# A two-block transformer kernel: the ends of the first block's layers worked by token tile, with a new order of weight loads

## The reference, cut to what matters

```python
for l in range(DEPTH):                       # DEPTH = 2
    h = rms_norm(x, pre_norm_g[l])           # x * rsqrt(mean(x*x) + 1e-6) * g
    u = jnp.einsum('bsd,de->bse', h, w_in[l])
    u_mla, u_sb, u_moba, u_conv, u_gate = jnp.split(u, SPLITS, axis=-1)
    ...                                      # MLA, stick-breaking and MoBA attention, a convolution of 31 taps
    y = jnp.concatenate([o_a, o_b, o_c, o_d], axis=-1) * jax.nn.silu(u_gate)
    y = jnp.einsum('bse,ed->bsd', y, w_out[l])
    x = x + rms_norm(y, post_norm_g[l])
```

```python
c_act = jax.nn.silu(c)
mods = jnp.split(c_act @ w_ada[i] + b_ada[i], 6, axis=-1)
u = x * (1.0 + sc1) + sh1
```

## Time and profile before

| | us |
|---|---|
| median of 3 runs (lowest, highest) | 1155.36 (1154.93, 1157.49) |
| the profiled execution | 1159.07 |
| its span, first to last instruction | 1156.6 |
| TensorE busy in the span | 1077.7 (93%) |
| VectorE busy | 448.8 (39%) |
| ScalarE busy | 167.5 (14%) |
| mean granted clock of TensorE | 0.968 |

### The profile page before, as it was taken

The page is one execution under the profiler, slowest core; times in us unless marked ns, Lnnn a source line. Parts: engine busy times, 40 slices in busy tenths (PEclk is TensorE's granted clock), DMA queues, the critical chain, the costliest instruction groups (busy, mean ns, idle before and its releaser), DMA issues. The chain is left out here.

```text
span 1156.6 us, 11866 instructions
## 1 busy us (share of the span) xinstructions
PE 1077.7 (93%) x4214; PEld 739.2 (64%) x4214; DVE 448.8 (39%) x1111; ACT 167.5 (14%) x402; POOL 25.1 (2%) x42
## 2 busy tenths in 40 slices
PE   3999994999999998997999999999999799999993
PEld 2758752758756857645666666678885466666661
DVE  2495625495725242537333333363322600000005
ACT  1124211124211231101000000002231000000000
POOL 2000000000000000000200000000000000000000
PEclk9999997999998999998999999979999899999997
DMA  6554454554465353345866555625332344444440
GB/s 246 218 207 181 161 216 161 218 195 182 168 218 218 146 218 146 108 183 190 303 231 239 218 218 220 232 93 182 109 116 103 114 177 154 164 153 145 145 145 36
DMA packets 29165, 204.58 MB, mean 177 GB/s; under 512 B 3423, under 2 KB 3460, under 8 KB 5453
## 3 DMA queue, kind: packets, MB, share of 16 engines
q1 hardware_dynamic: 26796, 191.60, 44.6%
q0 software_dynamic: 2336, 12.58, 2.9%
HBM read 203.11 MB, written 1.05 MB: 177 GB/s over the span
## 5 line engine op out<-in xcount | busy, mean ns | idle before, releaser
L1196 PE MATMUL bank<-hT,raw 128*128 128x256 f32 x2176 | 482.1, 380 | 2.9 <-DMA raw<-units_dram 2.4
L1196 PEld LDWEIGHTS bank<-hT,raw 128*128 128x128 f32 x2176 | 411.8, 190 | 77.0 <-issue 16.9
L1437 PE MATMUL bank<-raw,arena 128*128 128x512 f32 x512 | 224.6, 592 | 0.0
L1437 PEld LDWEIGHTS bank<-raw,arena 128*128 128x128 f32 x512 | 97.3, 190 | 109.7 <-issue 108.1
L1048 DVE TENSOR_TENSOR arena<-arena 128x512 f32<-128x512 f32 x32 | 23.8, 743 | 324.1 <-ACT arena L588 324.1
L1206 PE MATMUL bank<-raw,yT 128*128 128x512 f32 x224 | 99.4, 602 | 2.3 <-DVE yT L1108 2.0
L996 DVE SCALAR_TENSOR_TENSOR ada<-raw,cact,ada 128x256 f32 (+1 forms) x168 | 82.3, 490 | 6.0
L1206 PE MATMUL bank<-raw,hT 128*128 128x512 f32 (+1 forms) x192 | 76.7, 559 | 2.4 <-DVE hT L794 2.4
L1206 PEld LDWEIGHTS bank<-raw,yT 128*128 128x128 f32 x224 | 42.8, 193 | 55.3 <-issue 52.9
L588 ACT ACTIVATE arena<-bank 128x512 f32<-128x512 f32 x32 | 19.1, 597 | 397.8 <-PE bank L1196 397.8
L1206 PEld LDWEIGHTS bank<-raw,hT 128*128 128x128 f32 x192 | 37.2, 195 | 40.4 <-issue 34.7
(11 more groups left out here) (250 smaller groups left out, 714.1 us busy)
## 6 DMA issues: line engine op xcount, KB each, us to landing
raw<-units_dram SPq DMA_DIRECT2D x180, 1024.0 KB, 4.8
arena<-ln_rows_dram POOLq DMA_DIRECT2D x4, 1024.0 KB, 5.9
arena<-ada_rows_dram POOLq DMA_DIRECT2D x1, 2048.0 KB, 7.4
arena<-att_line_dram POOLq DMA_DIRECT2D x1, 2048.0 KB, 14.7
arena<-small_dram POOLq DMA_DIRECT2D x2, 896.0 KB, 6.5
xt<-x_dram SPq DMA_DIRECT2D x1, 1024.0 KB, 5.0
arena<-post_g_dram POOLq DMA_DIRECT2D x2, 512.0 KB, 8.8
out_dram<-xt SPq DMA_DIRECT2D x1, 1024.0 KB, 4.0
```

The lines of the kernel that those rows point to most:

```text
L1196: mm = pe.matmul(b[:, c * S:(c + 1) * S], raw[:, s, k * 256 + c * P:k * 256 + (c + 1) * P], act_t[:, k, :], start=(k == 0), stop=(k == KC ...
L1437: mm = pe.matmul(G[2 * h + t][:], hid[:, k, c, t * P:(t + 1) * P], raw[:, n % SLOTS, c * D + h * 512:c * D + (h + 1) * 512], start=False, ...
```

## The change

The order of units changes, and SP loads in another order at the start:

```diff
-ORDER = "wwawawwawwawawwa" "wawawawa" "wwawwa"
+ORDER = "wwwawwawwawawawa" "wawawawa" "awwwwa"
...
-            sp.dma_start(xt[:], x.rearrange("a (t p) d -> p (a t) d", p=P)).then_inc(x_in, 16)
-            sp.dma_start(kst[:], consts).then_inc(const_in, 16)
-            sp.dma_start(oneh[:], onehot).then_inc(rel_in, 16)
-            sp.dma_start(cact[:], ccol).then_inc(rel_in, 16)
+            sp.dma_start(cact[:], ccol).then_inc(ccol_in, 16)
+            sp.dma_start(xt[:, 0, :], x[0, 0:P, :]).then_inc(x_in[0], 16)
+            sp.dma_start(ident, consts[:, K_ID:K_ID + P]).then_inc(ident_in, 16)
+            sp.dma_start(xt[:, 1, :], x[0, P:S, :]).then_inc(x_in[1], 16)
+            sp.dma_start(oneh[:], onehot).then_inc(rel_in, 16)
             for s in range(SLOTS):
                 sp.dma_start(raw[:, s, :], units[s, :, :]).then_inc(landed[s], 16)
+            sp.dma_start(kst[:, P:], consts[:, P:]).then_inc(const_in, 16)
```

POOL's loads of the layer vectors (col, sm, gb) now wait for the first layer's `xs`; the gain of the first norm has a small tensor of its own, `pre`. The root on VectorE becomes four small instructions behind a root by ACT, one tile at a time:

```diff
+            def root_of(ssq, root):
+                ch.do(dve.tensor_scalar(neg[:], ssq, -0.5 / D, -0.5 * EPS, ALU.mult, ALU.add))
+                ch.do(dve.reciprocal(inv[:], root))
+                ch.sync()
+                ch.do(dve.tensor_scalar(err[:], inv[:], inv[:], neg[:], ALU.mult, ALU.mult))
+                ch.sync()
+                ch.do(dve.tensor_scalar(rst[:], err[:], 1.5, inv[:], ALU.add, ALU.mult))
+                ch.sync()
...
-                ada_unit(l, 0)
...
+                ada_unit(l, 0)
                 ada_unit(l, 1)
...
+                for t in range(NT):
+                    wait_output(dve, l, t)
+                    dve.wait_ge(osq_ready.sem, osq_ready.at(l, t + 1))
+                    ch.do(dve.tensor_tensor(xs[:, t, :], OY[t], gb[:], ALU.mult))
+                    dve.wait_ge(sso_ready.sem, sso_ready.at(l, t + 1))
+                    root_of(ssy[:, t:t + 1], root_y[:, t:t + 1])
+                    dve.scalar_tensor_tensor(xt[:, t, :], xs[:, t, :], rst[:], xt[:, t, :], ALU.mult,
+                                             ALU.add).then_inc(x_new.sem, 1)
```

`OY[t]` is one tile's output over two neighbouring banks. TensorE does the last two output units, the transposes and the first two units by tile, and multiplies zeros while it waits:

```diff
+            def zero_work(b, n):
+                for _ in range(n):
+                    pe.matmul(b[:], zeros[:, 0:P], zeros[:], start=True, stop=True)
...
+            def last_units(l):
+                for u in (U_O2, U_O3):
+                    wait_landed(pe, T1 * l, u)
+                for t in range(NT):
+                    for i, u in enumerate((U_O2, U_O3)):
+                        for k in range(4):
+                            mm = pe.matmul(OB[i][t][:], yT[:, 4 + k, t * P:(t + 1) * P],
+                                           raw[:, u % SLOTS, k * 512:(k + 1) * 512], start=False, stop=(k == 3))
+                        if t == 1:
+                            mm.then_inc(used[u % SLOTS], 1)
+                        elif i == 1:
+                            mm.then_inc(o_ready.sem, 1)
+
+            pe.wait_ge(zeros_ready, 1)
+            zero_work(G[0], 10)
...
             with pe.Fori(0, DEPTH) as l:
-                pe.wait_ge(xs_ready.sem, xs_ready.at(l, 2))
...
+                zero_work(A[0], 18)
+                first_transposes(l, 0)
+                first_units(l, 0)
+                first_transposes(l, 1)
+                first_units(l, 1)
```

More of the change, by code:

```diff
@@ L395, in _ @@
             for l in range(1, DEPTH):
+                pre_columns(l)
                 layer_vectors(l)
@@ L588, in relu_group @@
                 act.activation(relu[:, k], A[k][:], ACT.Relu).then_inc(relu_ready.sem, 1)
-            stage_input(0)
+            act.wait_ge(coef_ready.sem, coef_ready.at(0, 1))
+            for t in range(NT):
+                act.wait_ge(t0_ready, 2 * t + 1)
+                for c in range(4):
+                    act.activation(hT[:, c, t * P:(t + 1) * P], UB[t][0][:, c * P:(c + 1) * P], ACT.Identity,
+                                   scale=ucoef[:, 0, 0, c:c + 1], bias=ucoef[:, 0, 1, c:c + 1]).then_inc(u0_act, 1)
             act.wait_ge(lowp_ready, 1)
@@ new lines, in _ @@
+                    dve.tensor_scalar(xs[:, t, :], xt[:, t, :], rst[:], None, ALU.mult).then_inc(xs_ready.sem, 1)
+                dve.wait_ge(pre_in.sem, pre_in.at(l, 16))
+                for t in range(NT):
+                    dve.wait_ge(htp_ready.sem, htp_ready.at(l, 2 * t + 2))
+                    for i in range(4):
+                        c = 4 + i
+                        dve.tensor_scalar(hT[:, c, t * P:(t + 1) * P], HB[t][1][:, i * P:(i + 1) * P],
+                                          pre[:, c:c + 1], None, ALU.mult).then_inc(ht_dve.sem, 1)
@@ L1051, in _ @@
             coefficients(0)
-            stage_input(0)
+            for t in range(NT):
+                dve.wait_ge(t0_ready, 2 * t + 2)
+                for i in range(4):
+                    c = 4 + i
+                    dve.tensor_scalar(hT[:, c, t * P:(t + 1) * P], UB[t][1][:, i * P:(i + 1) * P], ucoef[:, 0, 0, c:c + 1],
+                                      ucoef[:, 0, 1, c:c + 1], ALU.mult, ALU.add).then_inc(u0_dve, 1)
             gate_rows(0)
@@ L1232, in values, with first_units @@
                 pe.matmul(o[:, c + P:c + S], v1, probsT[:, j % 2, S:384], start=False, stop=True).then_inc(pv_ready.sem, 1)
-            pe.wait_ge(rel_in, 32)
+            def zero_work(b, n):
+                for _ in range(n):
+                    pe.matmul(b[:], zeros[:, 0:P], zeros[:], start=True, stop=True)
+            def first_units(l, t):
+                for half, u in enumerate((U_MLA0, U_MLA1)):
+                    wait_landed(pe, T1 * l, u)
+                    for k in range(4):
+                        ht = ht_dve if half else ht_act
+                        pe.wait_ge(ht.sem, ht.at(l, 4 * t + k + 1))
+                        mm = pe.matmul(A[t][:, 0:MLA_IN], hT[:, 4 * half + k, t * P:(t + 1) * P],
+                                       raw[:, u % SLOTS, k * 512:k * 512 + MLA_IN],
+                                       start=(half == 0 and k == 0), stop=(half == 1 and k == 3))
+                    if t == NT - 1:
+                        mm.then_inc(used[u % SLOTS], 1)
@@ new lines, in first_transposes @@
+            def first_transposes(l, t):
+                pe.wait_ge(xs_ready.sem, xs_ready.at(l, t + 1))
+                for q in range(2):
+                    for i in range(4):
+                        c = 4 * q + i
+                        mm = pe.transpose(HB[t][q][:, i * P:(i + 1) * P], xs[:, t, c * P:(c + 1) * P], ident)
+                    mm.then_inc(htp_ready.sem, 1)
+            def last_units(l):
+                for u in (U_O2, U_O3):
+                    wait_landed(pe, T1 * l, u)
+                for t in range(NT):
+                    for i, u in enumerate((U_O2, U_O3)):
+                        for k in range(4):
+                            mm = pe.matmul(OB[i][t][:], yT[:, 4 + k, t * P:(t + 1) * P],
+                                           raw[:, u % SLOTS, k * 512:(k + 1) * 512], start=False, stop=(k == 3))
+                        if t == 1:
+                            mm.then_inc(used[u % SLOTS], 1)
+                        elif i == 1:
+                            mm.then_inc(o_ready.sem, 1)
@@ L1454, in net @@
                 second_product(s, 0, n0 + 1 + 5 * per, GROUPS - 1, 0, True)
-            modulation(0)
-            pe.wait_ge(x_new.sem, 2 * DEPTH + 2)
-            stage_input(0, xt)
+            modulation_columns(0)
+            for t in range(NT):
+                pe.wait_ge(x_new.sem, 2 * DEPTH + t + 1)
+                for q in range(2):
+                    for i in range(4):
+                        c = 4 * q + i
+                        mm = pe.transpose(UB[t][q][:, i * P:(i + 1) * P], xt[:, t, c * P:(c + 1) * P], ident)
+                    mm.then_inc(t0_ready, 1)
+            modulation_rows(0)
             pe.wait_ge(gla_in, 32)
-            pe.wait_ge(u_dve.sem, 4)
+            pe.wait_ge(u0_act, 8)
+            pe.wait_ge(u0_dve, 8)
             for k in range(KC):
-                wait_input(0, k)
                 mm = pe.matmul(A[1][0:16, 0:S], wlow[:, k, :], hT[:, k, :], start=(k == 0), stop=(k == KC - 1))
```

170 lines of the change are left out of this document (83 added, 87 removed).

## The result

The changed kernel takes 1185.26 us (median of 4 runs, 1181.5 to 1185.98) against 1155.14 us for the kernel before beside it (4 runs, 1154.69 to 1157.49): ratio 1.0256, 95% interval 1.0234 to 1.0278. It is slower, as forecast, and by 17 us more than forecast. The profiled execution is 1184.92 us, its span 1183.1 us, against 1156.6 us before: 26.5 us longer.

A forecast was written before the change was run, and what follows sets the result against it. TensorE's work was taken to bound each layer's body, with stops at the start and between layers. -10.2 - 11.4 - 2.6 + 30.4 + 6.4 = +12.6 gave 1171.7 profiled, 1168 us as median; range 1159 to 1175.

The forecast's parts named there:

- Start: Before the first layer's unit CA: it starts at 25.2 instead of 35.41 us, -10.2, bounds -11.6 and -5.4.
- Between the layers: From the output product to the next CA: +18.0 us instead of 29.8, taken as -11.4, bounds -12.5 and -8.5.
- Into the second block: From the columns' start to L1465: 17.0 to 18.0 us instead of 19.3, taken as -2.6, bounds -3.2 and -1.3.
- Order of units, waits: In the layers' bodies, TensorE waits 8.2 (nl), 2.6 (O0), 4.8 us (O2, O3): +30.4 for two layers, 29.3 to 31.5.
- Clock: Half clock behind the new waits in the bodies: 3.2 us a layer, +6.4 in all, 3 to 11.
- From profile to median: The profiled execution before lay 3.7 us above its median; that difference was applied, taking 1171.7 to 1168.
- the ends don't shrink as told: Rival: half clock between the layers and a start gaining only 5.4 us; +23.8, 1179 us. Chance of both 0.07, one 0.15.
- the five bounds: The bounds given with the five summed terms; the likeliest case was said to run from +5 to +24 us.

The follow-up runs named there:

- e2: The changed kernel with the order of units of the kernel before: 1171.38 us, ratio 1.0126.
- e8: The changed kernel with products of zeros ahead of the three waits in each layer's body: 1171.41 us, ratio 1.0146.
- e6: The changed kernel with the mended order of units, and O3's landing waited for only before its own first product: 1141.53 us, ratio 0.9874.
- e12: The kernel before with nothing but the mended order of units: 1153.86 us, ratio 0.9992.
- e1: The kernel before with nothing but the change's new order of units: 1187.32 us, ratio 1.0276.
- e5: The changed kernel with the mended order, VectorE's loop over the layers written out, and O3 waited for only before its own first product: 1135.63 us, ratio 0.9824.
- e11: As e5, but with 6 products of zeros instead of 18 ahead of each layer's first transposes: 1134.84 us, ratio 0.9809.
- e3: The changed kernel with the mended order of units (a2 ahead of V0, a3 unit 9, a10 behind O0): 1150.76 us, ratio 0.995.
- e10: As e7, with POOL's loads of the layer's vectors also held until both xs of that layer are written: 1186.04 us.
- e7: The changed kernel, with VectorE waiting for the next layer's third unit to land before its loop jumps back: 1188.82 us.
- e9: The changed kernel without the 18 products of zeros ahead of each layer's first transposes: 1184.67 us, ratio 1.0239.
- e4: The changed kernel with VectorE's loop over the two layers written out: 1176.59 us, ratio 1.0166.

## Why the prediction was right in its sign and wrong in its size

- *Start*: forecast -10.2, measured 35.41 to 25.70, **-9.7**. The one-hot product came at 7.59 (7.5 forecast), the zeros took 5.75 (3.9 to 7.8) and ended last, as told. (On the 35.41, see the last point.)
- *Between the layers*: forecast -11.4, measured 29.84 to 25.34, **-4.5**. This is the step that failed. "After that VectorE does tile 0's root and scaling" passed over the jump of VectorE's loop, which the change brings onto the path: before, ACT's square had to run there anyway; now the square of tile 0 is done early and VectorE's next instruction is the path. Written out, the stretch is 17.9 us (18.0 forecast before the allowance for the clock). Over the 18.4 of the sum the gap is 5.3 us; half clock behind the longer stop took 2.2, where 0.4 was allowed.
- *Into the second block*: forecast -2.6, measured **-0.35**. The steps went as told (no wait at the L1465 of before, L1560 now), but the clock fell earlier within the columns, 11.27 for 9.34, which the sum left out; where it fell later (e2, e8) the entry is 19.2, -3.7. The term was too large by its own sum as well: 17.0 to 18.0 against 19.3 is -1.3 to -2.3, not -2.6.
- *Order of units, waits*: forecast +30.4. The three waits were forecast at 8.2, 2.6 and 4.8 and measured at 8.12, 2.64 and 4.73, and e8 leaves 15.5 and 14.9 us over the old bodies: **+30.4**. The account through slots and queue was right, and not by luck: counted from CA, VectorE got a2 at +28.3 and a3 at +45.4, and TensorE's transposes went on at +71.8, against +28.5, +45.5 and +71.9. Its heading was not: e2 shows that the wait for O2 and O3 comes also with the old order (5.0 and 5.2), since the products by token tile want O3 earlier and the code waits for both units at once; with the mended order a wait for each unit removes it (e6).
- *Clock*: forecast +6.4 (3 to 11), measured 165.44 + 165.67 less 144.27, 144.17 and 30.4: **+12.3**, of which e8 takes back 12.5. This is the second step that failed. The mechanism was right and the size half: the short stops were put at 0.65 each, and the rows show 1.7 behind 2.64 (O0, 8.83 for 7.13) and 2.7 behind 4.73. Twice the loss is the time at half clock: 3.4 and 5.4 us, longer than the stops themselves.
- *From profile to median*: I carried 3.7 us from the profiled execution of before over to the median. The profiled execution after lies at its median (1184.92 and 1185.26), so this added 4.0 to the miss. That execution of before lies above all its others (1154.69 to 1157.49). The rows show where: its first units ran partly at half pace. First MLA0 and MLA1 of before, then of e12, which has the old code there:

```profile
23.73 11.50 PE L1206 MATMUL bank<-raw,hT 128*128 128x352 f32 x32 [1.17 <-DVE hT L794]
```
```profile
23.94 9.73 PE L1206 MATMUL bank<-raw,hT 128*128 128x352 f32 x32 [1.48 <-DVE hT L794]
```

In e1 and e12 CA starts at 33.2 and 33.5 and the entry is 21.2, against 35.4 and 22.9 in before. Measured against them the start gained 7.5 to 7.8 us and the entry lost 1.3. With one profile of each kernel this is a hint and no more, since their order of units differs.

The parts of the miss in the span: between the layers 6.9, clock 5.9, entry 2.3, start 0.5, the rest of the program -1.6: with rounding the 13.9 of 26.5 - 12.6. With the 4.0 above, less 0.6 (an execution is 2.5 us longer than its span before and 1.8 after), that is the 17 us of the medians. The rival "the ends don't shrink as told" had the nearest time (1179) and named half clock between the layers; it was the jump, and half clock behind it, so that its nearness is mostly luck.

The range was narrower than its own terms. The poor ends of the five bounds add up to -5.4 - 8.5 - 1.3 + 31.5 + 11 = +27.3, not to +24, and the range of 1159 to 1175 stops at +19.6. The measured +26.5 lies just under their sum, and three of the five terms lie beyond their own poor ends: between the layers (-4.5 against -8.5), the entry (-0.35 against -1.3) and the clock (12.3 against 11).

Of the rule of the Trainium skill ("TensorE: Matmul & The Clock Gate", section "Part 4: PE-mode transpose") that a transpose does not count as the array being busy in the same way, the runs decide little: with 18 products of zeros and a stop of 2.14 us (e5), the transposes and the products behind them ran at full clock, and with 6 and a stop of 4.73 (e11) at half. The transposes were the same in both; the zeros and the stop ahead of them differed.

## What to carry to other kernels

Where units stream through a ring of few slots in one queue, an order of loads and the moments at which the work wants them are one design: change either and follow every unit again (issue when its slot is free and all ahead of it in the queue are issued, landing, use). A code change that halves the time between two units' first uses needs a wait for each of them, not one for both (with the mended order, e6 against e3).

Before a shorter step is booked as a gain, ask what its engine does right there besides arithmetic: a loop's jump hidden behind another engine's work becomes a cost when that work is moved away. And price a new stop in a full body with its clock: here some 15 us of new stops made a layer 21.2 to 21.5 us longer, and where a stop can't be removed, work on zeros inside it gave those 6 back.

## What the runs showed of the hardware

- A loop's jump on VectorE: 3.8 us from the release to the next instruction with idle transfers (e10), 6.2 with transfers at 335 GB/s in that stretch (e7). In e2, e7 and e10 the next instruction follows a packet of the instruction queue by 1.9 to 2.1 us, in after, e3, e6 and e9 by 2.8. Gaps of 5.26 to 5.57 us in after, e2, e3, e6, e8 and e9; none with the loop written out (e4, e5, e11).
- Short stops of TensorE in the bodies of the first block did not all have the same effect. Of twelve stops of 2.5 to 2.8 us ahead of O0 (after, e1, e4, e7, e9, e10) ten were followed by half clock (1.2 GHz), with 8.83 us for 7.13, and two were not (layer 1 of e1 and of e4). Of four stops of 2.2 to 2.4 us ahead of the last products three were (e1 twice, e3 once). All twelve stops of 4.7 to 5.2 us there were, with 15.67 to 16.70 us for 13.9. A stop of 2.14 us behind zeros was not (e4 and e5).
- A product of zeros, 512 columns in bf16, took 0.225 us at full clock (18 in 4.05).
- Products of one column ran at half pace at half clock: sixty-four took 9.06 us where the clock fell after 5.0 us, and 11.27 where it fell after 2.6. An estimate from these two is 7 us for all of them at full clock; none of the fourteen profiles has that.
